# Triangular inverses of the DeltaNet chunks: matrix and transpose carried in packed form through every level

## What is computed

```python
a_mat = jnp.where(strict, bc[..., :, None] * kk * decay, 0.0) + jnp.eye(CHUNK)
rhs = jnp.concatenate([bc[..., None] * vc, (bc * jnp.exp(gc))[..., None] * kc], axis=-1)
sol = lax.linalg.triangular_solve(a_mat, rhs, left_side=True, lower=True, unit_diagonal=True)
```

## Time and profile before

| | |
|---|---|
| median of 3 runs | 1556.33 us (1556.08 to 1559.58) |
| profiled execution | 1557.05 us, span of the trace 1555.2 us |
| PE busy over the span | 95% |
| make stage, DVE's first product taken to its last subtraction | 829.06 to 999.99 us |
| of that stretch (829 to 1000): PE, DVE, ACT, POOL busy | 137.4, 130.0, 68.6, 88.4 us |
| TensorE clock granted there | 0.79 of full on average, 1.00 in the scan behind it |

### The profile page before, as it was taken

One profiled execution on the slowest core, in us unless ns is written; L12 is line 12 of the kernel. 1 busy time (PEld: TensorE's weight loads), 2 busy tenths in 40 slices (PEclk: granted clock), 3 DMA queues, 4 the chain that ended last, 5 costly groups with the idle time before them and its releaser, 6 DMA issues.

```text
span 1555.2 us, 29812 instructions
## 1 busy us (share of the span) xinstructions
PE 1477.3 (95%) x11798; PEld 1373.2 (88%) x11798; DVE 1043.3 (67%) x1943; ACT 601.4 (39%) x1180; POOL 154.1 (10%) x148
## 2 busy tenths in 40 slices
PE   6899999999999999999997878899999999999998
PEld 2799999999999999987785667899999999998886
DVE  4977777787365757553877887678887777753333
ACT  4522222221123533443556434354544444444223
POOL 0000000000000000020003545764000000000000
PEclk9999999999999999999996878999999999999999
DMA  9345444545244312211102100012123222221222
GB/s 341 102 144 151 142 152 149 154 143 161 82 149 136 96 46 77 59 55 42 42 2 62 43 30 16 22 53 71 55 59 91 81 81 86 81 77 69 81 68 95
DMA packets 174582, 141.85 MB, mean 91 GB/s; under 512 B 8464, under 2 KB 156437, under 8 KB 173461
## 3 DMA queue, kind: packets, MB, share of 16 engines
q1 hardware_dynamic: 151652, 117.89, 24.4%
q10 hardware_dynamic: 22833, 22.59, 4.6%
HBM read 137.01 MB, written 3.45 MB: 90 GB/s over the span
## 4 chain that ended last, share of the span: by engine, by line
PE 83%; DVE 10%; issue 3%; ACT 2%; SPq 1%; DMA 1%; POOL 0%; DVEq 0%; ACTq 0%
PE ps L2326 15%; PE ps L2328 14%; PE ps L2327 14%; PE ps L2478 5%; PE ps L2476 5%; PE ps L2477 5%; PE ps L2548 3%; PE ps L2547 3%; PE ps L2546 3%; PE ps L2756 1%; PE ps L2879 1%; PE ps L2909 1%; PE ps L2777 1%; PE ps L2923 1%; PE ps L3001 1%
## 5 line engine op out<-in xcount | busy, mean ns | idle before, releaser
L2326 PE MATMUL ps<-h_hi,w_lo 128*128 128x320 f32 x1152 | 364.7, 317 | 11.7 <-DVE h_lo L1429 4.5
L2328 PE MATMUL ps<-h_hi,w_hi 128*128 128x320 f32 x1152 | 356.9, 310 | 0.0
L2327 PE MATMUL ps<-h_lo,w_hi 128*128 128x320 f32 x1152 | 356.9, 310 | 0.0
L1382 DVE TENSOR_TENSOR w_lo<-w_raw,w_hi 128x1024 fp32r<-128x1024 f32 x120 | 147.7, 1233 | 228.9 <-ACT w_hi L748 228.6
L2326 PEld LDWEIGHTS ps<-h_hi,w_lo 128*128 128x128 f32 x1152 | 217.4, 189 | 18.5 <-DVE h_lo L1429 7.2
L2327 PEld LDWEIGHTS ps<-h_lo,w_hi 128*128 128x128 f32 x1152 | 217.6, 189 | 0.8 <-issue 0.2
L2328 PEld LDWEIGHTS ps<-h_hi,w_hi 128*128 128x128 f32 x1152 | 217.2, 189 | 0.0
L748 ACT CAST w_hi<-w_raw 128x1024 fp32r<-128x1024 f32 x120 | 125.6, 1048 | 197.3 <-PE ps L2328 107.8
L1516 DVE SCALAR_TENSOR_TENSOR ada_acc<-ada_ffn,cond,ada_acc 128x256 f32<-128x256 f32 x392 | 161.7, 478 | 1.2
L2326 PE MATMUL ps<-act_hi,w_lo 128*128 128x320 f32 (+1 forms) x352 | 108.9, 309 | 2.1 <-DVE mods L1545 2.1
L2328 PE MATMUL ps<-act_hi,w_hi 128*128 128x320 f32 (+1 forms) x352 | 108.5, 308 | 0.0
(11 more groups left out here) (413 smaller groups left out, 3015.8 us busy)
## 6 DMA issues: line engine op xcount, KB each, us to landing
w_raw<-in_w_ffn_in SPq DMA_DIRECT2D x64, 512.0 KB, 3.8
w_raw<-in_w_ffn_out SPq DMA_DIRECT2D x44, 512.0 KB, 3.8
ada_ffn<-in_w_ada ACTq DMA_DIRECT2D x43, 512.0 KB, 4.0
w_raw<-in_w_in SPq DMA_DIRECT2D x28, 512.0 KB, 3.7
...
```

Of the source, the lines that this page charges most:

```text
L1382: nc.vector.tensor_tensor(w_lo[at], w_raw[s][:], w_hi[at].bitcast(F32), ALU.subtract)\
L2326: nc.tensor.matmul(out, lo, xh, start=start, stop=False)
L2327: nc.tensor.matmul(out, hi, xl, start=False, stop=False)
L2328: return nc.tensor.matmul(out, hi, xh, start=False, stop=stop)
```

## The change

Level 1 to 4 now keep T and its transpose side by side in one tile (`t_pair`, 256 columns). PE computes both the product and the product of the transposes (32 blocks instead of 16, `inner_second`), so that DVE subtracts and masks both at once (L2109 and L2112 of the new kernel, 256 columns) and no longer transposes at every level; one transpose at the start is left. POOL's copies go. Level 5 is made of 32x32 block products off the diagonal (`outer_first`, `outer_second`, `outer_turned`; `outer_own` brings T's own blocks into PSUM by a product with the identity), level 6 of 64x64 ones (`last_first`, `last_second`). ACT takes over the evictions between them (steps 16 and 18), and ACT and DVE write the parts of `t_all` (18 and 19). The keys' products of all four heads are issued in one piece, the even and odd heads into different banks. A unit has 20 steps, the stage 64 cycles. The waits of those who use a unit's result are now on DVE and on ACT. SP's wait for `t_cols` is three signals earlier. In the last cycles ACT's scan preparation stands inside the loop; `w_low(TILE_WOUT, 0)` stands one cycle earlier. Below, most removed lines are left out, since the functions above show them.

```diff
-PE_T, DVE_T, ACT_T, POOL_T = 17, 28, 5, 8
+PE_T, DVE_T, ACT_T, POOL_T = 15, 21, 8, 1
-MAKE_STAGES = 21
-MAKE_START = [0, 4, 8, 13, 21, 25, 29, 34, 42, 46]
+MAKE_STAGES = 20
+MAKE_START = [0, 4, 8, 13, 20, 24, 28, 33, 40, 44]
...
-                        sp.wait_ge(t_pe[c], r * PE_T - d)
+                        sp.wait_ge(t_pe[c], r * PE_T - 4 * d)
...
+                    if c == THREE_DONE + 1:
+                        act.wait_ge(kv_copied, 2 * NT + 2)
+                        for b in range(4):
+                            scan_kg(0, b)
+                    if c in (THREE_DONE + 2, THREE_DONE + 3):
+                        for i in range(2 * (c - THREE_DONE - 2), 2 * (c - THREE_DONE - 1)):
+                            nc.scalar.activation(z_t[:, i, :], z_t[:, i, :], ACT.Silu)
+                    if c == THREE_DONE + 3:
+                        load_power_table()
+                    if THREE_DONE + 4 <= c < THREE_DONE + 8:
+                        scan_first(c - THREE_DONE - 4)
...
+                if k == 16:
+                    act.wait_ge(t_pe[c], r * PE_T + 10)
+                    nc.scalar.activation(x_w[c][:, 2, :], ps[:, 2 * c, 0:P], ACT.Copy, scale=-1.0).then_inc(t_act[c], 1)
+                if k == 18:
+                    act.wait_ge(t_pe[c], r * PE_T + 14)
+                    nc.scalar.activation(x_w[c][:, 2:4, :].rearrange("p a n -> p (a n)"), ps[:, 2 * c, 0:256],
+                                         ACT.Copy, scale=-1.0).then_inc(t_act[c], 1)
+                    act.wait_ge(t_dve[c], r * DVE_T + 20)
+                    for a in range(0, P, DK):
+                        ins = nc.scalar.copy(heads4(t_all[a:a + DK, t, g, :], P)[:, :, a:a + DK],
+                                             heads4(ps[a:a + DK, 2 * c + 1, 256:512], DK))
+                    ins.then_inc(t_act[c], 1)
...
+                    dve.wait_ge(t_pe[c], pe0 + 1)
                     dve.wait_ge(t_pool[c], r * POOL_T + 1)
...
+                    for_heads = [x.rearrange("p (h e) n -> p e h n", e=2)
+                                 for x in (m_t[c][:], tt_cols[c][:], heads4(p_all[:, t, g, :], P), x_w[c][:])]
+                    nc.vector.tensor_tensor(for_heads[0], ps[:, bank:bank + 2, 0:256].rearrange("p e (h n) -> p e h n", n=P),
+                                            for_heads[1], ALU.mult).then_inc(t_dve[c], 1)
                 if k == 7:
...
+                    dve.wait_ge(t_act[c], act0 + 5)
+                    nc.vector.transpose(x_w[c][:, 0, :], x_w[c][:, 1, :]).then_inc(t_dve[c], 1)
                     dve.wait_ge(t_dve[c], dve0 + 4)
...
+                    nc.vector.tensor_tensor(subs(t_pair), subs(m_pair), packed("level0", 8), ALU.mult).then_inc(t_dve[c], 1)
+                    dve.wait_ge(t_dve[c], dve0 + 5)
+                    nc.vector.tensor_tensor(subs(t_pair), subs(t_pair), packed("ident", 8), ALU.add).then_inc(t_dve[c], 1)
                 n, part = divmod(k - 6, 2)
                 if 1 <= n <= 4 and part == 0:
...
+                    dve.wait_ge(t_pe[c], pe0 + 2 * n)
+                    nc.vector.tensor_tensor(heads4(x_c, SUB), heads4(ps[:, bank, 0:P], SUB), packed(f"level{n}", 4),
+                                            ALU.mult).then_inc(t_dve[c], 1)
                 if 1 <= n <= 4 and part == 1:
...
+                    dve.wait_ge(t_pe[c], pe0 + 1 + 2 * n)
+                    nc.vector.tensor_tensor(t_pair, t_pair, heads4(ps[:, bank + 1, 0:256], P), ALU.subtract).then_inc(t_dve[c], 1)
                 if 0 <= n <= 4 and part == 1:
...
+                    dve.wait_ge(t_dve[c], dve0 + 6 + 3 * n)
+                    nc.vector.tensor_tensor(subs(t_sides), subs(t_pair), packed(f"sides{n + 1}", 8), ALU.mult).then_inc(t_dve[c], 1)
+                if k == 17:
+                    dve.wait_ge(t_pe[c], pe0 + 13)
+                    half6 = const("half6")[:, None, 0:DK].broadcast_to([P, 8, DK])
+                    nc.vector.tensor_tensor(tt_cols[c][:].rearrange("p a n -> p (a n)").rearrange("p (h n) -> p h n", n=DK),
+                                            heads4(ps[:, bank + 1, :], DK), half6, ALU.mult).then_inc(t_dve[c], 1)
+                if k == 19:
                     dve.wait_ge(t_pe[c], pe0 + 15)
...
+                    for a in range(0, P, DK):
+                        ins = nc.vector.tensor_copy(heads4(t_all[a:a + DK, t, g, :], P)[:, :, DK - a:2 * DK - a],
+                                                    heads4(ps[a:a + DK, bank, 256:512], DK))
+                    ins.then_inc(t_dve[c], 1)
...
+            def products(t, g, c):
+                for at, which in ((0, 4), (256, 0)):
+                    for h in range(4):
+                        out = ps[:, 2 * c + h % 2, at + (h // 2) * P:at + (h // 2 + 1) * P]
+                        ins = nc.tensor.matmul(out, qk(t, g, h, 4), qk(t, g, h, which), start=True, stop=True)
                 ins.then_inc(t_pe[c], 1)
...
+            def blocks_of(x, a, h):
+                return x[a:a + SUB, h * SUB:(h + 1) * SUB]
+            def inner_first(c):
                 for h in range(4):
...
+                    for a in range(0, P, SUB):
+                        ins = nc.tensor.matmul(blocks_of(ps[:, 2 * c, 0:P], a, h), blocks_of(x_w[c][:, 1, :], a, h),
+                                               blocks_of(tt_cols[c][:, 0, :], a, h), start=True, stop=True)
                 ins.then_inc(t_pe[c], 1)
...
+            def inner_second(c):
+                x, tt = x_w[c][:, 2, :], tt_cols[c][:, 1, :]
+                for i, (lhs, rhs) in enumerate(((tt, x), (x, tt))):
+                    for h in range(4):
+                        for a in range(0, P, SUB):
+                            ins = nc.tensor.matmul(blocks_of(ps[:, 2 * c + 1, i * P:(i + 1) * P], a, h), blocks_of(lhs, a, h),
+                                                   blocks_of(rhs, a, h), start=True, stop=True)
+                ins.then_inc(t_pe[c], 1)
+            def outer_first(c):
                 for h in range(4):
...
                     for a in range(0, P, SUB):
...
+                        o = a ^ SUB
+                        ins = nc.tensor.matmul(blocks_of(ps[:, 2 * c, 0:P], o, h), m_t[c][a:a + SUB, h, o:o + SUB],
+                                               blocks_of(tt_cols[c][:, 0, :], a, h), start=True, stop=True)
+                ins.then_inc(t_pe[c], 1)
+            def pair_block(c, i, a, h, half):
+                at = i * 256 + h * DK + half * SUB
+                return ps[a:a + SUB, 2 * c + 1, at:at + SUB]
+            def outer_own(c):
+                for i in range(2):
+                    for h in range(4):
+                        for a in range(0, P, SUB):
+                            ins = nc.tensor.matmul(pair_block(c, i, a, h, a // SUB % 2), blocks_of(t_cols[c][:, 1 - i, :], a, h),
+                                                   unit_ident(a), start=True, stop=True)
+                ins.then_inc(t_pe[c], 1)
+            def outer_second(c):
+                for h in range(4):
+                    for a in range(0, P, SUB):
+                        ins = nc.tensor.matmul(pair_block(c, 1, a ^ SUB, h, a // SUB % 2), blocks_of(x_w[c][:, 2, :], a, h),
+                                               blocks_of(tt_cols[c][:, 1, :], a, h), start=True, stop=True)
+                ins.then_inc(t_pe[c], 1)
+            def outer_turned(c):
+                for h in range(4):
+                    for a in range(0, P, SUB):
+                        ins = nc.tensor.matmul(pair_block(c, 0, a, h, 1 - a // SUB % 2), blocks_of(tt_cols[c][:, 1, :], a, h),
+                                               blocks_of(x_w[c][:, 2, :], a, h), start=True, stop=True)
+                ins.then_inc(t_pe[c], 1)
+            def sides6(c, i, a, h):
+                return tt_cols[c][a:a + DK, 2 * i + h // 2, h % 2 * DK:(h % 2 + 1) * DK]
+            def last_first(c):
+                for h in range(4):
+                    for a in (0, DK):
+                        o = DK - a
+                        ins = nc.tensor.matmul(ps[o:o + DK, 2 * c, h * DK:(h + 1) * DK], m_t[c][a:a + DK, h, o:o + DK],
+                                               sides6(c, 0, a, h), start=True, stop=True)
+                ins.then_inc(t_pe[c], 1)
+            def last_second(c):
+                for h in range(4):
+                    for a in (0, DK):
+                        o = DK - a
+                        ins = nc.tensor.matmul(ps[o:o + DK, 2 * c, 256 + h * DK:256 + (h + 1) * DK],
+                                               x_w[c][a:a + DK, 2 + h // 2, h % 2 * DK:(h % 2 + 1) * DK],
+                                               sides6(c, 1, a, h), start=True, stop=True)
                 ins.then_inc(t_pe[c], 1)
...
+                    products(t, g, c)
                 n, part = divmod(k - 6, 2)
                 if 1 <= n <= 4 and part == 0:
...
+                    pe.wait_ge(t_dve[c], dve0 + 4 + 3 * n)
+                    inner_first(c)
```

(17 more changed lines are left out.)

183 lines of the change are left out of this document (50 added, 133 removed).

## The result

| | before | after |
|---|---|---|
| median | 1557.95 us (4 runs, 1556.08 to 1560.92) | 1589.51 us (4 runs, 1586.65 to 1591.03) |
| ratio | | 1.0194, 95% interval 1.0174 to 1.0213 |
| span of the profiled execution | 1555.2 us | 1588.1 us |
| make stage (DVE's first masked product to its last write) | 170.2 us | 202.0 us |
| rest of the span, behind the stage | 555.9 us | 555.6 us |

The account below looks back on a forecast made before the run. DVE was taken to bound the make stage at full clock, PE at the halved one. Mixed cycles of 142 us plus ACT's part made 143.5 against 170.2, so 26.7 off 1557.05 gave 1530.4, forecast 1530 us, range 1508 to 1549.

Parts of the forecast that it names:

- The frame: Make stage and scan: the scan keeps its 56 us, and whatever the make stage saves is handed on whole.
- DVE's prices: Make stage, DVE's time per instruction: 0.41 us a 256-wide subtraction, 0.43 a 256-wide mask; 9.6 us a unit against 13.6.
- PE's prices: Make stage, PE's weight-load times per group: keys 1.9 or 1.05 us, 64x64 sets 1.0 or 0.55, at low or full clock.
- The change on PE: Make stage, PE's work for four units: 50.0 us at the low clock and 31.0 at full, from 59.1 and 33.7.
- The sum for 58 cycles: Make stage from cycle 5 to its end: 147 us at the low clock, 117 at full, 142 mixed, against 170.
- the end of the stage: Make stage's start and end, with fewer units: scaled by the factor 0.96 found in the kernel before.
- the test on the kernel before: Make stage's repeating part: summing each cycle's larger engine time gave 62.4 us against 61.0 measured, called 2% high.
- The clock: Make stage: granted clock 0.50 for five sixths of it; a rival with full clock for half or more, 1502 to 1518, chance 0.2.
- The blocks off the diagonal run one by one: Rival, levels 5 and 6 on PE: such products don't overlap, 5.9 us a unit more, 1589 us; chance 0.07.
- ACT becomes a link that waits: Rival, make stage: PE stands behind ACT's L1290 and L1293 of other units, 1547 us; chance 0.13.
- my signs of failure: Make stage: L2887 or L2906 over 0.7, PE waiting long for L1290 or L1293, or clock 1.00 for half the stage.
- changes of shape: Make stage, PE's tiling switches: 120 before, 67 now; 12 us more gain, 1518, if each of 53 counted; left out.

Follow-up runs that it names:

- the rows: 512 extra unread 32x32 products put ahead of the first unit's level 1 in the kernel before; on the diagonal 29 us, off it 28.1 us.
- the kernel with wide products: Kernel after, but in levels 1 to 4 and level 5's first product four heads become one 32x32 by 32x128 product: 1537.65 us, ratio 0.9843.
- both: Kernel after, with one product a level and DVE's transposes back, and ACT instead of PE writing T's own blocks into PSUM: 1551.25 us, ratio 0.9946.
- the row off the diagonal: Kernel before with 512 extra unread 32x32 products from rows a to rows a ^ 32, ahead of the first unit's level 1: the row took 28.1 us.

## Why the prediction was wrong, step by step

**The frame held.** The scan took what it took before, and the stage's loss was handed on whole. DVE's prices held: 0.42 for the 256-wide subtraction (0.41 forecast), 0.29 for the level's product, but 0.51 and 0.46 for the 256-wide mask, where I had 0.43 between 0.30 and 0.68. Lines of DVE against the earlier trace rows:

```profile
L2112 DVE TENSOR_TENSOR tt_cols<-t_cols,cst 128x256 f32<-128x256 f32 x30 | 15.4, 513 | 1.0
L2109 DVE TENSOR_TENSOR t_cols<-t_cols,ps 128x256 f32<-128x256 f32 x24 | 10.1, 421 | 27.6 <-PE ps L2879 27.4
L2105 DVE TENSOR_TENSOR x_w<-ps,cst 128x128 f32<-128x128 f32 x24 | 6.7, 288 | 15.3 <-PE ps L2870 15.1
```

In the last column is the new order of things: DVE waits for PE.

**PE's prices held too**, group by group, where no stop for instructions fell into a group, at the low clock and at the full one (compare):

```profile
839.95 1.78 PEld L2861 LDWEIGHTS ps<-pre 64*128 64x128 f32 x16
...
864.78 0.93 PEld L2924 LDWEIGHTS ps<-tt_cols,m_t 64*64 64x64 f32 x16
...
902.77 0.64 PEld L2879 LDWEIGHTS ps<-spare 32*32 32x32 f32 x64 [1.01 <-DVE spare L2105]
...
932.49 0.37 PEld L2906 LDWEIGHTS ps<-tt_cols,x_w 32*32 32x32 f32 x32
...
959.27 0.55 PEld L2932 LDWEIGHTS ps<-tt_cols,x_w 64*64 64x64 f32 x16
...
966.93 0.55 PEld L2906 LDWEIGHTS ps<-spare 32*32 32x32 f32 x32
```

1.78 for the keys (1.9 forecast), 0.93 and 0.55 for the 64x64 sets (1.0 and 0.55), 0.64 for 32 blocks, and L2906 with 0.55 at the low clock and 0.37 at the full one for its 16 blocks off the diagonal (L2913, on it, has 0.52 above). Every price of PE was right to about a tenth of a microsecond, and the sum was wrong, because it had **one price too few**.

**The step that failed** is "The change on PE": it adds up what each group takes to run and leaves out what it takes to bring the instructions. Per unit the change goes from 156 products to 296, four instructions each, and in the rows a block of 256 took 3.45 us or more, however little it does. The sum for 58 cycles gave 142 us, with 47 blocks in it: 47 x 3.45 = 162 us, and still 154 at 3.28, the shortest distance between two transfers in any trace here. The stage that I forecast could not be supplied. The count of instructions was at hand, and so were the 25 transfers of the stage before; the price of one was not, since the kernel before never ran long enough on small products to be stopped (its longest gap inside them is 0.3). Its shortest distance between two transfers, 3.42 us, was in the trace, and the sum made no use of it. The first 40 cycles took 138.7 us, 41 more than the 40 x 2.45 of the forecast. 36.3 us of "issue" stand in them, against 4.1 in the kernel with wide products, so some 32 of the 41 are the supply; what the other 9 are is not shown. The kernel with wide products took 96.0 us for these cycles (2.40 a cycle against my 2.45), though its cheaper running and higher clock have a share in that.

**The second error is the end of the stage.** I took the last 18 cycles as cheaper than the mean by the change's whole factor, 44 us. With the supply out of the way they took 56.8 us; before, the last 19 took 54.1. PE was busy 44.66 us of the last 55 before, and 45.35 of the last 57 in the wide kernel: what stands in these cycles is the scan's first step and pieces of the output projection, which the change doesn't shorten, and at the low clock a load of them takes 0.33 us instead of 0.19 (mean of one). That cost 12.7 us. The other 6.5 in after's 63.3 are not assigned: PE's loads have as little "issue" there (5.1 us) as in the wide kernel (5.9), 2.2 and 2.6 of it at a piece of the output projection, so it is hardly the supply; the clock is lower (0.65 against 0.71) and narrow products cost more to run. Windows of the kernel before, and of the kernel after with wide products:

```profile
945.00:1000.00 55.00, 44.66 (x816) 39.72 (x816) 35.02 (x73) 20.74 (x59) 33.84 (x32) 0.84 0.05 16
```

```profile
930.00:987.00 57.00, 45.35 (x884) 37.17 (x883) 27.85 (x58) 23.01 (x68) 18.03 (x13) 0.71 0.06 16
```

Together: 40.7 + 12.7 + 6.5, less the 1.5 that I had added for ACT, are the 58.4 us between 143.5 and 202.0; of these the supply is shown for some 32, the end of the stage for 12.7.

**A slip and a miscount** are in the working too. In the test on the kernel before, 34% of low clock between 58.6 and 71.4 make 62.9 and not 62.4, so the method was 3% high and not 2%; that would have taken 1 to 2 us off the forecast. And "48 blocks off the diagonal" a unit are 32: the 16 of `outer_turned` (L2913) go from rows a to rows a.

**The clock** was forecast at 0.50 for five sixths of the stage, 118 us; it was 72% of 202, 145 us. The direction was right. It costs more than I gave it: the forecast had 117 us at the full clock and 147 at the low one, 0.2 for each us, and the runs have 0.3. In the kernel **both**, 60 us more at the low clock than before are, by that estimate, 18 us of time, and most of what it gains at equal clock (1563 to 1538) goes there.

**The rivals.** "The blocks off the diagonal run one by one" gave 1589 and the time was 1589.5. The number fits by accident: its mechanism is refuted by L2906 at 0.55 and by the row off the diagonal, and with the right count of 32 blocks its own sum (2.8 + 1.7 us a unit, less 27) would have been 1575. "ACT becomes a link that waits" is not what happened either: no row of PE's loads waits for L1290 or L1293. None of my rivals was about the supply, and my signs of failure (L2887 or L2906 over 0.7, PE waiting for ACT, the clock full for half of the stage) would not have named it: three of the twenty sets of L2887 and L2906 did take longer, 1.7 to 2.9 us, but by a stop inside them. What the rivals had in common was that they knew only an engine's work and its waits for other engines.

**On changes of shape**, which I left out of the sum: after changes shape as often with wide products as with narrow ones (66 times), and the first 40 cycles with wide products came to 96.0 us where the sum without such a term has 98. No term for it shows there, though wide products are also cheaper to run and the clock was 0.71, so a small one could hide.
